# A third pair of gate matrices by seven block products instead of eight, with its added preparation placed on GpSimd and moved on VectorE

## What is computed

```python
def hybrid_layer(x, ...):
    h = rms_norm(x, norm_g)
    z = h @ w_in
    (x_rnn, g_rnn, sc_b, sc_c, x_sc, g_sc, c_q, c_kv, k_rope, g_att, gate_logits) = jnp.split(z, idx, axis=-1)
    y_rnn = (rg_lru(x_rnn, ...) * jax.nn.silu(g_rnn)) @ rg_out
    y_sc = (sc_b * causal_depthwise_conv(sc_c * x_sc, sc_conv_w) * jax.nn.silu(g_sc)) @ sc_out
    y_att = (mla(c_q, c_kv, k_rope, ...) * jax.nn.silu(g_att)) @ mla_out
    gates = jax.nn.sigmoid(gate_logits + gate_b.reshape(-1)).reshape(b_, t_, 3, 1024)
    merged = gates[:, :, 0] * y_rnn + gates[:, :, 1] * y_sc + gates[:, :, 2] * y_att
    return x + merged @ w_out
```

## Time and profile before

| | us |
|---|---|
| median of three runs | 1694.24 |
| lowest and highest of them | 1694.19, 1695.64 |
| the profiled execution: its time | 1694.07 |
| the profiled execution: span from first to last instruction | 1692.3 |
| outside the span (1694.07 - 1692.3) | 1.8 |
| mean granted clock of TensorE | 0.999 |

### The profile page before, as it was taken

The page is one execution under the profiler, slowest core; times in us unless marked ns, Lnnn a source line. Parts: engine busy times, 40 slices in busy tenths (PEclk is TensorE's granted clock), DMA queues, the critical chain, the costliest instruction groups (busy, mean ns, idle before and its releaser), DMA issues.

```text
span 1692.3 us, 31902 instructions
## 1 busy us (share of the span) xinstructions
PE 1668.8 (99%) x11840; PEld 1565.3 (92%) x11840; DVE 1126.7 (67%) x1563; ACT 578.3 (34%) x1037; POOL 1249.5 (74%) x1345
## 2 busy tenths in 40 slices
PE   7999999999999999999999999999999999999999
PEld 7999999999999999999998888898889998889887
DVE  7965758485666687767359657484846666887751
ACT  5423333342333424323135233333324334233320
POOL 7764848385888787878867748484858996989874
PEclk9999999999999999999999999999999999999999
DMA  4432212222222233322532322231322232233234
GB/s 156 146 99 63 93 63 91 67 83 92 94 88 87 87 101 101 115 89 74 195 122 80 108 63 95 72 99 60 89 93 86 88 98 98 91 112 98 90 109 155
DMA packets 50295, 164.50 MB, mean 97 GB/s; under 512 B 6144, under 2 KB 7552, under 8 KB 50176
## 3 DMA queue, kind: packets, MB, share of 16 engines
q1 hardware_dynamic: 42192, 146.56, 27.1%
q10 hardware_dynamic: 8032, 17.00, 2.9%
HBM read 152.21 MB, written 10.81 MB: 96 GB/s over the span
## 4 chain that ended last, share of the span: by engine, by line
PE 79%; DVE 10%; POOL 4%; DMA 3%; issue 3%; ACT 1%; SPq 0%; DVEq 0%; ACTq 0%; POOLq 0%
PE slots L626 63%; PE slots L899 5%; PE slots L691 3%; PE slots L725 3%; DVE weight_sums L1804 2%; DMA w_raw<-w_units 2%; POOL w_lo L489 2%; PE slots L787 2%; POOL w_lo L563 2%; PE slots L709 1%; DVE early L1530 1%; POOL w_hi L484 1%; DVE early L1545 1%; PE slots L660 1%; ACT w_hi L1274 1%
## 5 line engine op out<-in xcount | busy, mean ns | idle before, releaser
L489 POOL TENSOR_TENSOR w_lo<-w_raw,w_hi 128x256 fp32r<-128x256 f32 x860 | 754.1, 906 | 17.9
L484 POOL TENSOR_SCALAR w_hi<-w_raw 128x1024 fp32r<-128x1024 f32 x215 | 259.1, 1205 | 230.6 <-PE slots L626 195.3
L626 PE MATMUL slots<-h_hi,w_hi 128*128 128x264 f32 (+1 forms) x1680 | 405.3, 308 | 0.7 <-DVE sc_pad L1658 0.7
L626 PE MATMUL slots<-h_lo,w_hi 128*128 128x264 f32 (+1 forms) x1680 | 399.8, 305 | 0.0
L626 PE MATMUL slots<-h_hi,w_lo 128*128 128x264 f32 (+1 forms) x1680 | 399.5, 304 | 0.0
L626 PEld LDWEIGHTS slots<-h_hi,w_hi 128*128 128x128 f32 x1680 | 270.9, 188 | 14.7 <-issue 1.6
L626 PEld LDWEIGHTS slots<-h_hi,w_lo 128*128 128x128 f32 x1680 | 270.1, 188 | 12.9
L626 PEld LDWEIGHTS slots<-h_lo,w_hi 128*128 128x128 f32 x1680 | 270.3, 188 | 12.1
L626 PE MATMUL slots<-branch_hi,w_hi 128*128 128x264 f32 (+1 forms) x552 | 144.1, 320 | 17.8 <-DVE branch_lo L1375 9.1
L626 PE MATMUL slots<-branch_lo,w_hi 128*128 128x264 f32 (+1 forms) x552 | 141.8, 316 | 0.0
L626 PE MATMUL slots<-branch_hi,w_lo 128*128 128x264 f32 (+1 forms) x552 | 141.6, 316 | 0.0
(11 more groups left out here) (276 smaller groups left out, 3713.4 us busy)
## 6 DMA issues: line engine op xcount, KB each, us to landing
w_raw<-w_units SPq DMA_DIRECT2D x251, 512.0 KB, 3.5
stream<-sc_acc ACTq DMA_DIRECT2D x16, 264.0 KB, 2.1
sc_back<-stream SPq DMA_DIRECT2D x8, 528.0 KB, 3.5
x_old<-stream SPq DMA_DIRECT2D x16, 264.0 KB, 4.7
stream<-residual_or_merged ACTq DMA_DIRECT2D x16, 264.0 KB, 3.3
ab_raw<-w_units SPq DMA_DIRECT2D x8, 512.0 KB, 4.1
residual_or_merged<-xt ACTq DMA_DIRECT2D x4, 528.0 KB, 7.5
stream<-xt ACTq DMA_DIRECT2D x1, 2112.0 KB, 9.6
```

Source lines behind the costliest of these rows:

```text
L484: pool.tensor_scalar(hi, raw, 1.0, 1.0, ALU.mult, ALU.mult).then_inc(sem("hi_part"), 1)
L489: op = pool.tensor_tensor(lo[:, cols], raw[:, cols], hi[:, cols].bitcast(F32), ALU.subtract)
L626: mm = pe.matmul(out[:, a_, 0:t1 - t0], w(k), x(k)[:, t0:t1], start=(n == 0), stop=(n == 3 * ks - 1))
```

## The change

- `PLAIN` goes from 3 to 2: pair 2 ("a" of turn 1) goes by seven products as well, in both layers. What belongs to it follows by the code: two splits fewer on GpSimd and one `lead` more, one `weight_sums`, one `pair_sums` and one set of casts more on VectorE and ScalarE, and one step fewer of `gates` on ScalarE. Of the 96 matmuls of 264 columns of that pair in layer 0, 84 remain; of 48 with 512 columns in layer 1, 84 with 256.
- The eight additions `h_again` of a layer move from VectorE to GpSimd, into a new function `whole_h`. The first four stand between the split of pair 0 and that of the first y unit, behind a wait for the recurrent branch's last block products and for `in_x`; the other four behind the split of y0 of turn 0, and wait for `rnn_full` too.
- VectorE's list at the head of `MR` is reordered: mixes 0, 1, lower 0, mixes 2, lower 1, `att_gate(0)`, mixes 3, lower 2, the weight sums of the first pair by seven, `merge` of y0, lower 3.
- ScalarE's list: `branch_upper(0)` and `mix_upper(2)` come ahead of `gates(1)`; `mix_upper(3)` stands between `gates(1)` and the first `lead_upper`.

```diff
-PLAIN = 3
+PLAIN = 2
...
+                def whole_h(i):
+
+                    pool.wait_ge(*at("rg_mm", l, 3, 4))
+                    pool.wait_ge(*at("in_x", l, 3, 2))
+                    if i > 1:
+                        pool.wait_ge(*at("rnn_full", l, 3, i - 1))
+                    for n in range(2):
+                        pool.tensor_tensor(tile(mix_whole, i)[:, n * T:(n + 1) * T], tile(h_hi, i + 4 * n).bitcast(F32),
+                                           tile(h_lo, i + 4 * n).bitcast(F32), ALU.add).then_inc(sem("h_again"), 1)
+
                 split_pair(0)
+                whole_h(0)
+                whole_h(1)
                 for i in range(4):
                     split_unit("MR", l, i, 2, 2)
                     if i:
                         branch_lower(i - 1)
+                    else:
+                        whole_h(2)
+                        whole_h(3)
...
                 gates(0)
                 mix_upper(0)
                 mix_upper(1)
-                gates(1)
                 branch_upper(0)
                 mix_upper(2)
+                gates(1)
                 mix_upper(3)
-                gates(2)
                 for n in range(4):
                     lead_upper(0, n)
...
                     whole, mixed = tile(mix_whole, i), tile(mix_full, i)
-                    for n in range(2):
-                        dve.tensor_tensor(whole[:, n * T:(n + 1) * T], tile(h_hi, i + 4 * n).bitcast(F32),
-                                          tile(h_lo, i + 4 * n).bitcast(F32), ALU.add).then_inc(sem("h_again"), 1)
                     dve.wait_ge(*at("h_again", l, i, 2))
...
                 mixes(0)
                 mixes(1)
+                mixes_lower(0)
+                mixes(2)
+                mixes_lower(1)
                 att_gate(0)
-                mixes_lower(0)
-                mixes_lower(1)
-                mixes(2)
+                mixes(3)
+                mixes_lower(2)
+                weight_sums(0)
                 merge("MR", 0, 0)
-                mixes_lower(2)
-                merge("MR", 0, 1)
-                mixes(3)
-                weight_sums(0)
                 mixes_lower(3)
-                att_gate(1)
```

## The result

| | before | changed |
|---|---|---|
| median, us | 1694.19 (1692.84 to 1695.64) | 1701.87 (1700.38 to 1703.13) |
| ratio to before, 95% interval | | 1.0045 (1.0031 to 1.0060) |
| profiled execution, span, clock | 1694.07, 1692.3, 0.999 | 1703.07, 1700.9, 0.997 |

The forecast was 1692.5 us, at the most 1695.0.

A forecast was written before the change was run, and what follows sets the result against it. TensorE, busy for 99% of the span, was taken to bound the kernel. Layer 0 gains 1.51 - 0.1 = 1.41, layer 1 1.23 - 0.3 - 0.6 = 0.33, so 1694.24 - 1.74 = 1692.5 us, range 1691.5 to 1693.6.

The forecast's parts named there:

- What bounds the kernel, and the gain: TensorE bounds; pair 2 by seven products in `MR` saves 1.51 us in layer 0, 1.23 in layer 1.
- The lead blocks of the new pair: GpSimd's lead remainders late for pair 2's fourth product: 0.3 us in layer 1 (0 to 0.6), 0 in layer 0.
- The pair behind it: Pair 3 gets pair 5's lateness: 0.6 us in layer 1 (0 to 1.14), 0.1 in layer 0 (0 to 0.13).
- What I cost at nothing: GpSimd's eight additions and VectorE's list ahead of pair 2's third product: 0 us, with about 1 us to spare.
- The cover that I named: Additions overrun GpSimd's idle gaps by 1.3 to 5.1 us; 4.7 us remain before TensorE asks for y1's split.
- at the worst: VectorE's last lower mix in layer 1 ends at 1463.5 without free pace; the third product wants it at 1461.2.
- Everything behind `MR` follows TensorE's own releases.: Stages after `MR` pass the gain through, at no cost.
- The slower rival: VectorE's last lower mix late for pair 2's third product, 4.7 us in layer 1, 3.7 in layer 0; 1699.9 us, chance 0.08.
- No new wait: Casts run ahead, VectorE leaves GpSimd alone, pair 3 is as good as pair 4; 1691.5 us, chance 0.14.
- the gain is eaten: Pair 3's loads land late, its work slips 1 us or more in both layers; about 1694.2 us, chance 0.18.
- The signs named at the end: Profile checks: pair 2's length and wait releaser, pair 3 of layer 1 at 15.5 to 16.6 us, GpSimd's and VectorE's finishing times.
- The last sign: If pair 2 gains but the span is not shorter, something behind `MR` does not follow TensorE; no size given.

The follow-up runs named there:

- experiment 3: The changed kernel with the additions of h's two parts back on VectorE, third pair by seven and new orders kept; 1700.14 us, ratio 1.0031.
- no_adds: The changed kernel without any additions of h's two parts, the mixes made of h's upper part alone; 1696.76 us, ratio 1.0009.
- 181 spares: The changed kernel with 181 spare wait instructions on TensorE behind products of layer 1's `MR`; 1697.99 us, ratio 1.0017.

## Why the prediction was wrong, step by step

- **What bounds the kernel, and the gain (2.74).** Right. Without the additions pair 2 takes 10.22 us in layer 0 and 10.00 in layer 1, where 10.22 and 9.88 were worked out.
- **The lead blocks of the new pair (0.3, at most 0.6).** In no_adds 10.00 - 9.88 = 0.1. With the additions the wait is 0.53 us in layer 1, within the range. In layer 0, where I took 0 and at most 0.2, pair 2 takes 0.84 more than its products and waits for nothing but these blocks.
- **The pair behind it (0.6 in layer 1, 0 to 1.14).** Right in place and at the far end in size: 1.16 us in no_adds, behind a wait of 0.60. That is pair 5's price, which I halved without a reason; pair 5 itself no longer pays it (10.15 us, 11.02 before), so it does not hang on following a pair by seven alone. In layer 0: nothing without the additions, 0.1 taken; 0.87 with them, outside the range of 0 to 0.13.
- **What I cost at nothing: the additions and VectorE's list.** This step failed: 1.7 us in layer 0, 3.0 in layer 1. GpSimd's additions took 6.21 and 6.71 us for four each in layer 1, 1.55 to 1.68 for one, inside the range that I had. The cover that I named, idle time on GpSimd, held for GpSimd, and y1's split was never late. It was VectorE that paid. Its recurrent tail in layer 1, before and after:

```profile
1418.21 1.33 DVE L1893 SCALAR_TENSOR_TENSOR decay_tanh<-decay_sq,decay_tanh 128x528 f32<-128x528 f32 x2 [2.71 <-ACT decay_sq L1236]
1420.70 0.71 DVE L1898 TENSOR_TENSOR i_gate<-decay_tanh,i_gate 128x528 f32<-128x528 f32 x1 [1.16 <-ACT decay_tanh L1240]
...
1428.82 0.69 DVE L1362 TENSOR_TENSOR rnn_lo<-decay_sq,rnn_hi 128x512 f32 x1 [0.33 <-ACT rnn_hi L1247]
```

```profile
1421.31 2.46 DVE L1904 SCALAR_TENSOR_TENSOR decay_tanh<-decay_sq,decay_tanh 128x528 f32<-128x528 f32 x2 [2.71 <-ACT decay_sq L1251]
1423.80 1.72 DVE L1909 TENSOR_TENSOR i_gate<-decay_tanh,i_gate 128x528 f32<-128x528 f32 x1
...
1432.49 3.55 DVE L1376 TENSOR_TENSOR rnn_lo<-decay_sq,rnn_hi 128x512 f32 x2
```

The tail ends at 1432.49 + 3.55 = 1436.04 against 1429.51, and the whole layer is 3.10 later: 3.4 us lost. I had bounded this by 4.8 and taken half of it, but in the rival alone; in the sum it was nothing. On VectorE the additions take the same room in the list instead (experiment 3), and so it made little difference where they stood. The Trainium skill, "SBUF — State Buffer", section "SBUF: two separate sides", has the port pair as an exclusive lock for a whole instruction. The trace agrees: beside an addition of 1.55 us a VectorE instruction of 0.71 became 1.72. Then the last lines ahead of the third product:

```profile
1461.73 1.22 DVE L1815 TENSOR_TENSOR weight_sums<-w_raw 128x512 f32<-128x512 f32 x1
1462.87 0.67 DVE L1764 SCALAR_TENSOR_TENSOR gated<-gate_tanh,slots 128x512 f32<-128x512 f32 x1
1463.58 1.20 DVE L1768 TENSOR_TENSOR residual_or_merged<-residual_or_merged,gated 128x512 f32<-128x512 f32 x1
1464.70 1.76 DVE L1798 TENSOR_TENSOR h_mixes_lo<-h_mixes,h_mixes_hi 128x1024 fp32r<-128x1024 f32 x1
```

1464.70 + 1.76 = 1466.46, and TensorE goes on at 1466.61. That is 5.03 us behind pair 2's start: the end that I had worked out "at the worst" (1463.5 - 1458.33 = 5.17), and not 1460 or earlier (1.7 behind it), on which the nothing in the sum rested. That it meets the worst case so well is luck: 3.4 us of it are the late start, which the worst case did not have, and the list itself went faster. In no_adds the same mix ends at 1455.39, 2.22 us ahead of pair 2. I had counted a free pace of VectorE up to the end of its list. It has it only until GpSimd's lead remainders begin (1459.38); from there 0.69 is 1.22, and 1.22 is 1.76.

VectorE's lateness reaches the lead blocks too, by two ways that the forecast did not have. In layer 1 the last mix cast, which stands ahead of the first lead cast, waited for VectorE, so that cast came at 1458.68, 0.91 us later against pair 2 than worked out. In layer 0 the first remainder came as early as in no_adds (3.4 us ahead of pair 2 in both), but VectorE's list still ran beside GpSimd's first six remainders, and they took 6.60 us where they take 4.77 in no_adds:

```profile
1457.72 1.06 ACT L1275 ACTIVATE h_mixes_hi<-h_mixes 128x1024 fp32r<-128x1024 f32 x1 [1.01 <-DVE h_mixes L1792]
...
624.10 6.60 POOL L563 TENSOR_TENSOR w_lo<-w_raw,w_hi 128x256 fp32r<-128x256 f32 x6 [6.57 <-ACT w_hi L1289]
```

- **"Everything behind `MR` follows TensorE's own releases."** Wrong, and I had weighed no case of it: 2.7 us in `MS` of layer 1. A pair of 84 matmuls in the place of 48, each of two instructions (weights and product), with 3 waits more, makes TensorE's program ahead of that stage 75 instructions longer (1629 against 1554 in the traces, from pair 0 on), and a 16 KB packet of its code then falls onto the first weight loads of `MS`.
- **The rivals.** The slower rival (0.08) had the right mechanism with the wrong price: 1.35 us for the lower mix, not 4.7, and none for it in layer 0. That its 1699.9 comes near the measured time is luck: the code fetch adds what it lacks. "No new wait" and "the gain is eaten" are both out.
- **The signs named at the end.** Pair 2 of layer 1 over 11 us, released by the lower mix: it came. Pair 3 up to pair 4 took 16.82 us, just over its 15.5 to 16.6. The last sign, pair 2's gain there and the span not shorter, came only in no_adds (10.00 us, span 1694.0); in the changed kernel the gain was gone too. What it warned of, something behind `MR` that does not follow TensorE, is true of both, and had no chance of its own.

What stays open: why a packet 0.3 us behind the first load delays the second by 0.8 us in one trace and 2.6 in another, and one 0.7 behind it by 0.5; and the exact rule by which a jump sets where blocks begin: with 181 spares the packet came off the loads, but to 0.3 us behind pair 8's start, where the kernel before has it 3.6 ahead.

## What to carry to other kernels

An operation moved to an idle engine is not free if the two engines slow each other, and moving it back does not help either: add up the work of both up to the first product that waits for it, and put that into the sum, not into a rival. With a later deadline the same additions cost nothing. If a change lengthens or shortens the program of the engine that bounds the kernel, look in the stages behind for where its code fetches fall among the loads; before a loss there is given to the change's idea, run it once with some spare instructions behind the last loop.
